# Two-layer block with routed experts on one core: the tensors behind the small constants moved by 32 bytes

## What is computed

```python
# first block, each of 2 layers
h = x @ w_in                                    # 1024 x 5280 columns
... three attentions (8, 8 and 4 heads) on pieces of h -> ya, yb, yc (512 wide each)
g = sigmoid(x @ w_m + b_m)                      # 1024 x 3072
merged = ga * (ya @ w_a) + gb * (yb @ w_b) + gc * (yc @ w_c)
r = ALPHA * x + merged @ w_o
x = layernorm(r + sigmoid(r @ w_pg) * (p @ w_p))
# second block: layer 0
x = x + hybrid_mixer(rmsnorm(x), w_in_2, ..., w_out_2)
x = x + swiglu(rmsnorm(x), w_gate, w_up, w_down)          # 2816 wide
# second block: layer 1
x = x + hybrid_mixer(...)
x = x + moe_swiglu(rmsnorm(x), router, w_gate, w_up, w_down)   # top 2 of 8 experts, 3584 wide each
x = rmsnorm(x)
```

## Time and profile before

| | |
|---|---|
| median of three runs | 2153.93 us (2153.34 to 2155.3) |
| the profiled execution, its own time | 2153.59 us |
| its span, first to last instruction | 2151.8 us, so 1.8 us lie around it |
| granted TensorE clock, mean of the span | 0.997 of full speed |
| HBM read | 525.84 MB, 245 GB/s over the span |

### The profile page before, as it was taken

One profiled execution on the slowest core, in us unless ns is written; L12 is line 12 of the kernel. 1 busy time (PEld: TensorE's weight loads), 2 busy tenths in 40 slices (PEclk: granted clock), 3 DMA queues, 4 the chain that ended last, 5 costly groups with the idle time before them and its releaser, 6 DMA issues.

```text
span 2151.8 us, 33474 instructions
## 1 busy us (share of the span) xinstructions
PE 2121.7 (99%) x13275; PEld 1891.3 (88%) x13275; DVE 1414.5 (66%) x1431; ACT 1294.8 (60%) x1427; POOL 650.3 (30%) x316
## 2 busy tenths in 40 slices
PE   9999999999999999999999999999999999999998
PEld 8979999988999898999998888888888888888887
DVE  1455223336413694223696999999999989899997
ACT  4556445455644544444554777777777777777776
POOL 5716885825788202888401000000000000000000
PEclk9999999999999999999999999999999999999999
DMA  7434554515455333565455999999999999999995
GB/s 243 134 110 150 170 195 145 178 56 174 155 181 184 105 124 128 187 194 176 139 177 158 377 376 349 361 356 377 357 348 371 361 375 343 352 360 376 366 360 208
DMA packets 307633, 529.06 MB, mean 246 GB/s; under 512 B 11842, under 2 KB 152802, under 8 KB 307520
## 3 DMA queue, kind: packets, MB, share of 16 engines
q1 hardware_dynamic: 306496, 525.92, 70.3%
q0 software_dynamic: 736, 1.00, 0.2%
q10 hardware_dynamic: 288, 0.52, 0.1%
HBM read 525.84 MB, written 1.05 MB: 245 GB/s over the span
## 4 chain that ended last, share of the span: by engine, by line
PE 86%; POOL 5%; DVE 4%; issue 2%; ACT 2%; DMA 0%; POOLq 0%; SPq 0%; DVEq 0%; ACTq 0%
PE bank L718 84%; POOL weights_low L3000 5%; PE bank L1459 1%; DVE qb L2268 1%; ACT sc L1599 1%; DVE sc L2268 1%; PE bank L891 0%; DVE sc L2276 0%; DMA ring<-in_w_ple_dram 0%; ACT weights_high L1602 0%; DVE nmax L2303 0%; DVE h L2276 0%; DVE y L2276 0%; ACT sq L1599 0%; ACT xT L1599 0%
## 5 line engine op out<-in xcount | busy, mean ns | idle before, releaser
L2268 DVE TENSOR_TENSOR expert_weights_low<-ring_experts,expert_weights_high 128x2048 fp32r<-128x2048 f32 x336 | 764.4, 2288 | 73.1 <-ACT expert_weights_high L1602 73.0
L1602 ACT ACTIVATE expert_weights_high<-ring_experts 128x2048 fp32r<-128x2048 f32 x336 | 644.0, 1917 | 168.1 <-PE bank L718 163.8
L3000 POOL TENSOR_TENSOR weights_low<-ring,weights_high 128x1024 fp32r<-128x1024 f32 x252 | 616.0, 2468 | 370.2 <-ACT weights_high L1602 370.2
L1602 ACT ACTIVATE weights_high<-ring 128x1024 fp32r<-128x1024 f32 x294 | 303.4, 1055 | 346.4 <-PE bank L718 304.6
L718 PE MATMUL bank<-x_high,weights_high 128*128 128x256 f32 x1024 | 289.1, 285 | 1.1 <-POOL weights_low L3000 1.1
L718 PE MATMUL bank<-x_high,weights_low 128*128 128x256 f32 x1024 | 283.0, 279 | 0.0
L718 PE MATMUL bank<-x_low,weights_high 128*128 128x256 f32 x1024 | 280.3, 283 | 0.0
L718 PE MATMUL bank<-h_high,weights_high 128*128 128x256 f32 x704 | 199.7, 286 | 5.4 <-ACT h_high L1602 5.4
L718 PE MATMUL bank<-h_high,weights_low 128*128 128x256 f32 x704 | 198.5, 284 | 0.0
L718 PEld LDWEIGHTS bank<-x_high,weights_high 128*128 128x128 f32 x1024 | 192.4, 188 | 2.6 <-DVE zs L2276 1.6
L718 PEld LDWEIGHTS bank<-x_high,weights_low 128*128 128x128 f32 x1024 | 194.4, 190 | 0.1
(11 more groups left out here) (331 smaller groups left out, 3825.1 us busy)
## 6 DMA issues: line engine op xcount, KB each, us to landing
ring_experts<-in_moe_w_gate_dram SPq DMA_DIRECT2D x112, 1024.0 KB, 6.7
ring_experts<-in_moe_w_up_dram SPq DMA_DIRECT2D x112, 1024.0 KB, 6.7
ring_experts<-in_moe_w_down_dram SPq DMA_DIRECT2D x112, 1024.0 KB, 6.4
ring<-in_w_in_dram SPq DMA_DIRECT2D x62, 1024.0 KB, 5.3
ring<-in_w_merge_dram SPq DMA_DIRECT2D x24, 1024.0 KB, 5.2
ring<-in_w_out_dram SPq DMA_DIRECT2D x14, 1024.0 KB, 5.4
ring<-in_ffn_w_gate_dram SPq DMA_DIRECT2D x11, 1024.0 KB, 5.3
ring<-in_ffn_w_up_dram SPq DMA_DIRECT2D x11, 1024.0 KB, 5.3
```

The costliest lines, as they stand in the source:

```text
L1602: return nc.scalar.activation(dst, src, ACT.Copy, scale=scale)
L2268: return nc.vector.tensor_tensor(dst, x, z, op)
L3000: nc.gpsimd.tensor_tensor(half_of(wlo[:, q_slot, :], t, width), half_of(ring[:, slot, :], t, width), half_of(whi[:, q_slot, :], t, width). ...
```

## The change

`eps` gets 16 columns in place of 3. It takes 64 bytes of a partition in place of 12, padded to 32, so every tensor allocated behind it lies 32 bytes further up. The program's instructions, their order on every engine, their waits and their shapes stay the same; only addresses differ.

```diff
--- before.py
+++ after.py
@@ -290,7 +290,7 @@
         m0.close()
         sq = sb("sq", [P, DT, S])
         ones = sb("ones", [P, 4, P])
-        eps = sb("eps", [P, 3])
+        eps = sb("eps", [P, 16])
         zeros = ctx.enter_context(nc.sbuf_tensor("zeros", [P, 512], mybir.dt.bfloat16))
         ident = cst[:, C_IDENT:C_IDENT + P]
         ONES = {D: ones[:, 0], Q_LORA: ones[:, 1], KV_LORA: ones[:, 2], P: ones[:, 3]}
```

## The result

The changed kernel took **2159.64 us** (median of 15 runs, 2154.39 to 2162.51) against 2153.97 us of the kernel before in as many runs: a ratio of **1.0025, 95% interval 1.0018 to 1.0032**. It is slower by 5.7 us, where 6.4 us less was forecast and the range ended at 2154.5 us. The profiled execution took 2159.34 us, with a span of 2157.5 us.

A forecast was written before the change was run, and what follows sets the result against it. The prediction took TensorE's split matmuls to bound the kernel; savings of 3.2 + 1.5 + 1.7 = 6.4 us took the profiled 2153.59 us to 2147.2, and with the median 0.3 us above, to 2147.5 us, range 2140 to 2154.5 us.

The forecast's parts named there:

- What bounds the kernel: Whole kernel: TensorE, busy 2121.7 of 2151.8 us, almost all split products, so a saving per matmul reaches the end one for one.
- What one matmul costs at which address: Split matmuls of 256 columns: 117.5 to 119.0 ns by operand remainders; all on multiples of 64 should give the best pace.
- the aligned row: Stretch with weights moving on a multiple of 64 and `x` stationary: 48 matmuls in 5.66 us, 117.9 ns each.
- the simple rule: Split matmuls: an operand 32 bytes off costs time; `pick`, with both operands off, took 117.5 ns and spoke against it.
- term 3: Expert matmuls of 512 columns: 0.42 ns less each over 4032, 1.7 us saved, with bounds from nothing to 8.5 us.
- sign of a wrong basis: Stretches of `h` and `x`: both should come to 117.9 ns a matmul; not coming together would show the basis wrong.
- Term 1: `x` products: 1.04 ns less for each of 3072 matmuls, 3.2 us saved, perhaps a little high.
- Term 2: `h`, `y`, `hidden`, `merged` products: 0.42 ns less for each of 3600 matmuls, 1.5 us saved.
- Rival A: Experts gain nothing, only the savings on the other products remain: 4.7 us, 2149.2 us; chance 0.25.
- Rival D: Experts: both operands at remainder 0 get in each other's way, 3.3 ns more a matmul, 13.3 us lost, 2162.5 us; chance 0.06.
- Terms 4 to 6: Tensors losing alignment, VectorE, ScalarE and GpSimd work, and feeding a faster TensorE: no cost or limit counted in the sum.
- The rule of 16-byte lines: SBUF reads: both placements are multiples of 16, so nothing would change and the time would stay 2153.9 us.

The follow-up runs named there:

- The one part undone: The changed kernel with 192 bytes ahead of `h_high`, so that `h_high` and `h_low` alone move to distance 192 from the weights: 2147.59 us, 0.9974 of the kernel before.
- the shift by 224: The kernel before with `eps` at 64 columns, everything behind it 224 bytes further up: 2138.82 us, ratio 0.9932.

## Why the prediction was wrong

- **What bounds the kernel**: right. TensorE's busy time moved, the others' did not, and every nanosecond on a split matmul of thousands went into the end.
- **What one matmul costs at which address**: this is the step that failed. "Either way the three pairings of the first and second block come, after the change, to stand as the aligned row does" took the remainder of each tensor for the cause. The aligned row has its weights moving past `x_high`, at a distance of 64, and past `x_low`, at 32. The pairs of `h` came to distance 0, which no row of 256 columns showed. The row that spoke against the simple rule, `pick`, lies at distance 64 too, at which `h` later ran at 117.7 ns. It was noted and used for a bound of term 3, but not for what `h` would come to. The prediction's own sign of a wrong basis, that "`h` and `x` don't come together at one pace", is what came: 120.0 and 118.0 ns.
- **Term 1, `x`**: -3.2 us forecast, -2.4 us measured. The direction and about the size were right.
- **Term 2, `h`, `y`, `hidden`, `merged`**: -1.5 us forecast, +5.8 us measured. This term alone turns the sign: the pairs went from 118.3 to 120.0 ns and not to 117.9. The one part undone shows it in the other direction, by 12 us for `h` alone.
- **Term 3, the experts**: -1.7 us forecast, nothing measured. Rival A had this right; both operands moved together and their distance stayed 0. Its own time, 2149.2 us, was off by the same step as term 2.
- **Rival D** came nearest in kind: it has a cost that depends on how the two operands lie to each other, worst at equal remainders. It put it on the wrong family, and distance 96 is as slow as 0 for `h`. That the operands get in each other's way is not shown. Its argument against, that "weights and `x_high` both lie on multiples of 64 and run at the best pace", again looked at remainders by 64, where the two are 192 apart by 256. Its time, 2162.5 us, is near the 2159.64 us measured by luck: it has the loss in the experts, which lost nothing.
- **Terms 4 to 6**: right as far as seen. VectorE's and ScalarE's work on the expert weights stayed at 2289 and 1917 ns a piece.
- **The rule of 16-byte lines** (the Trainium skill, SBUF — State Buffer, Specifications) would have both placements alike. The runs don't agree: kernels that differ only in addresses that are all multiples of 16 reach from 2138.82 to 2178.91 us. The gap of N/2.4 + 2.5 ns that the Trainium skill gives for an isolated warm matmul (TensorE: Matmul & The Clock Gate, Back-to-back issue gap), an estimate of 109.2 ns at 256 columns, was not reached by the split matmuls of any of them; the best stands at 113.3.
- **The rest of the loss**, some 2 us of the 5.7, was not in the forecast. In the profiled pair 1.6 us of it are the clock, which is chance; between the medians it stays open.

## What to carry to other kernels

When matmuls with their own weight load run back to back in float32r, compare the start-to-start time of the same instruction at other addresses before believing in an alignment rule: what counts is the pair, moving against stationary, and a "rounder" address can be the worst. Shift one operand's tensor by 32 to 224 bytes and read the pace, in several stretches and not in one, since some distances have two. It costs one unused tensor; the best shift here, of everything behind `eps`, was worth 0.7%. Where a profile holds a row that breaks the rule one is about to use, as `pick` did here, the row belongs into the sum and not beside it.

## What the runs showed of the hardware

- Split matmuls of 256 columns run at 113.3 to 120.0 ns and those of 512 columns at 226.7 to 233.3 ns, at a granted clock of 1.00, depending on where the two operands lie to each other. The best distance for the one is among the worst for the other.
- Several of the steady paces are multiples of 3.33 ns, which is 8 clocks of 2.4 GHz: 113.3, 116.7, 120.0, 226.7, 233.3. Others are not: 117.7, 118.3, 118.8, 229.2, 232.5. No run shows what sets the paces, or how the two operands are read.
- A stream keeps a pace that its addresses alone don't fix. `x_high` against the weights, where no `x_low` lies between, is at unchanged offsets in the kernel before and the changed one. Before, 32 matmuls from the first row to the second:

```profile
324.56 0.28 PE L718 MATMUL bank<-x_high,weights_high 128*128 128x256 f32 x1
...
328.32 0.28 PE L718 MATMUL bank<-x_low,weights_high 128*128 128x256 f32 x1
```

In the changed kernel, 18 matmuls:

```profile
324.94 0.28 PE L718 MATMUL bank<-x_high,weights_high 128*128 128x256 f32 x1
...
326.98 0.28 PE L718 MATMUL bank<-x_high,weights_high 128*128 128x256 f32 x1
```

3.76/32 = 117.5 ns against 2.04/18 = 113.3 ns. Ahead of it runs the stream of `merged`, which had other offsets in the two kernels; that this is what picks the pace is not shown. What picks it, and whether a kernel can be made to take the fast one every time, stays open; at the shift by 224 it would be worth some 11 us by the means above.
